# Weight tiles between the steps of a dilated head: 2, 3, 2, 4 and 3 of them in place of 2 each

## What is computed

```
def dilated_layer(x, g, w_in, w_mem_kv, w_out, mem_n, kv):
    h = rmsnorm_2(x, g)
    parts = split_cols(h @ w_in, [DIL_W] * n_g + [DIL_W, MEM_W, MEM_W])
    gate_d, mq, gate_m = parts[n_g], parts[n_g + 1], parts[n_g + 2]
    for gi, (window, dil) in enumerate(DIL_CONFIG):
        q = parts[gi].reshape(B, S, DIL_HEADS, DIL_DH)
        o, lse = dilated_group(q, kv[2 * gi], kv[2 * gi + 1], dil, window // dil)
        outs.append(o); lses.append(lse)
    alpha = jax.nn.softmax(jnp.stack(lses, axis=0), axis=0)
    o = jnp.sum(alpha[..., None] * jnp.stack(outs, axis=0), axis=0)
    o_dil = o.reshape(B, S, DIL_W).astype(x.dtype) * jax.nn.silu(gate_d)
```

## Time and profile before

| | us |
|---|---|
| median of 3 runs | 4379.09 |
| lowest, highest | 4377.94, 4389.87 |
| the profiled execution, its own time | 4371.75 |
| its span in the trace | 4369.9 |
| PE busy | 4004.5 (92%) |
| PE weight loads busy (beside PE) | 3762.6 (86%) |
| ACT busy | 1564.4 (36%) |
| DVE busy | 1510.8 (35%) |
| POOL busy | 1351.6 (31%) |

### The profile page before, as it was taken

One profiled execution on the slowest core, in us unless ns is written; L12 is line 12 of the kernel. 1 busy time (PEld: TensorE's weight loads), 2 busy tenths in 40 slices (PEclk: granted clock), 3 DMA queues, 4 the chain that ended last, 5 costly groups with the idle time before them and its releaser, 6 DMA issues.

```text
span 4369.9 us, 95432 instructions
## 1 busy us (share of the span) xinstructions
PE 4004.5 (92%) x42564; PEld 3762.6 (86%) x42564; DVE 1510.8 (35%) x2011; ACT 1564.4 (36%) x1954; POOL 1351.6 (31%) x632
## 2 busy tenths in 40 slices
PE   6988999889897899999988999898999999999978
PEld 5876778788886899999988999797899999999978
DVE  2123224466655433332333233324222222222232
ACT  3332224521213343343433333334333333333333
POOL 2321113100002344444433344433333333333333
PEclk8999999999998999999999999999999999999989
DMA  5886665100003455555544444444544444445433
GB/s 210 298 287 237 245 229 176 55 4 4 4 10 111 140 183 183 180 188 183 181 145 147 146 154 150 137 158 142 172 158 157 164 149 146 160 157 166 145 123 133
DMA packets 181879, 668.39 MB, mean 153 GB/s; under 512 B 20288, under 2 KB 20288, under 8 KB 180704
## 3 DMA queue, kind: packets, MB, share of 16 engines
q1 hardware_dynamic: 175248, 642.07, 43.0%
q10 hardware_dynamic: 4944, 16.03, 1.1%
q0 software_dynamic: 1280, 4.20, 0.2%
HBM read 653.82 MB, written 8.39 MB: 152 GB/s over the span
## 4 chain that ended last, share of the span: by engine, by line
PE 83%; DVE 6%; ACT 4%; issue 3%; DMA 2%; POOL 1%; ACTq 0%; POOLq 0%; DVEq 0%; SPq 0%
PE ps L903 65%; PE ps L864 2%; PE ps L1144 2%; PE ps L1120 2%; ACT wh L1371 1%; PE ps L1056 1%; PE ps L1134 1%; DVE wl L1833 1%; PE ps L846 1%; PE ps L1359 1%; ACT halves L1371 1%; DMA raw<-in_w_k 1%; POOL wl L2375 1%; PE ps L1343 1%; ACT xw L1371 1%
## 5 line engine op out<-in xcount | busy, mean ns | idle before, releaser
L903 PE MATMUL ps<-halves,wh 128*128 128x256 f32 (+1 forms) x13632 | 2627.1, 294 | 99.3 <-POOL wl L2375 23.2
L903 PEld LDWEIGHTS ps<-halves,wh 128*128 128x128 f32 x13632 | 2185.4, 195 | 170.3 <-issue 80.0
L903 PE MATMUL ps<-halves,wl 128*128 128x256 f32 (+1 forms) x6816 | 1984.7, 291 | 0.0
L2375 POOL TENSOR_TENSOR wl<-raw,wh 128x1024 fp32r<-128x1024 f32 x508 | 1234.2, 2430 | 2121.1 <-ACT wh L1371 2120.8
L1371 ACT ACTIVATE wh<-raw 128x1024 fp32r<-128x1024 f32 x1016 | 1071.9, 1057 | 1493.1 <-PE ps L903 1181.7
L1833 DVE TENSOR_TENSOR wl<-raw,wh 128x1024 fp32r<-128x1024 f32 x508 | 688.4, 1356 | 1919.3 <-ACT wh L1371 1918.9
L903 PEld LDWEIGHTS ps<-halves,wl 128*128 128x128 f32 x6816 | 1328.2, 195 | 14.1
L903 PE MATMUL ps<-wh,halves 128*128 128x256 f32 x2688 | 499.3, 285 | 0.6 <-POOL wl L2375 0.6
L903 PEld LDWEIGHTS ps<-wh,halves 128*128 128x128 f32 x2688 | 424.3, 192 | 11.3 <-issue 8.1
L903 PE MATMUL ps<-wl,halves 128*128 128x256 f32 x1344 | 381.0, 283 | 0.0
L903 PEld LDWEIGHTS ps<-wl,halves 128*128 128x128 f32 x1344 | 258.8, 193 | 0.3
(11 more groups left out here) (243 smaller groups left out, 2488.0 us busy)
## 6 DMA issues: line engine op xcount, KB each, us to landing
raw<-in_ffn SPq DMA_DIRECT2D x264, 512.0 KB, 4.0
raw<-in_ada SPq DMA_DIRECT2D x192, 512.0 KB, 4.6
raw<-in_w_kv SPq DMA_DIRECT2D x192, 512.0 KB, 3.4
raw<-in_w_in_b SPq DMA_DIRECT2D x160, 512.0 KB, 3.9
raw<-in_w_in_a SPq DMA_DIRECT2D x128, 512.0 KB, 3.5
raw<-in_mem SPq DMA_DIRECT2D x64, 512.0 KB, 5.7
raw<-in_w_out_a SPq DMA_DIRECT2D x48, 512.0 KB, 4.0
raw<-in_w_out_b SPq DMA_DIRECT2D x48, 512.0 KB, 4.0
```

The source lines that it names most:

```text
L903: p = self.e.matmul(o, x, y, start=bi not in begun, stop=final and kc == 3 and m == 2, skip_group_check=True)
L2375: return self.e.tensor_tensor(out, a, b, op)
```

## The change

`pipeline_tight` no longer alternates two tiles and one step. A new function deals the tiles of the first seven results by a list of counts that it repeats: two ahead of step 1, three ahead of step 2, two ahead of step 3, four ahead of step 4, three ahead of step 5, and the same for the second head, 28 in all. Tiles, instructions, buffers and banks are the same.

```diff
+def weave(g, steps, counts):
+
+    for n in itertools.cycle(counts):
+        rest(limited(g, n))
+        if next(steps, "end") == "end":
+            break
+    rest(g)
@@
-                run_all((part(made[:7]), 2), (before, 1))
+                weave(part(made[:7]), before, (2, 3, 2, 4, 3))
                 rest(part(made[7:]))
```

## The result

| | before | with the change |
|---|---|---|
| median, us | 4378.51 (4 runs, 4375.6 to 4389.87) | 4351.53 (4 runs, 4348.59 to 4353.76) |
| ratio, 95% interval | | 0.9931 (0.9914 to 0.9948) |
| the profiled execution, its own time | 4371.75 | 4353.76 |
| its span | 4369.9 | 4352.0 |

The change makes the kernel faster: 27 us by the two medians, which is 0.62%, and 0.69% by the ratio in the table, which is not that of the medians. The forecast was 4350.5 us, 28.6 us less than before. Run again later the changed kernel gave 4352.27 us against 4383.85 (6 and 11 runs), a ratio of 0.9929 (0.9913 to 0.9945).

A forecast was written before the change was run, and what follows sets the result against it. TensorE, busy 92%, bounds the kernel, so only its gaps can yield time. 21.1 + 7.5 = 28.6 us off 4371.75 gives 4343.2; the median, 7.3 us above, gives 4350.5 us, range 4335 to 4372.

The forecast's parts named there:

- waits, 28: PE's waits before the transposes in seven pairs of dilated heads: 9.70 to 6.68 us a pair, 21.1 us gained.
- clock: Beside the seven pairs, half-clock stretches of 1.5 us each fall from seven to two: 7.5 us back.
- The late softmax: Dilated heads: softmax begins within the last tile before the transposes (waits 1.97, 2.88 us); more tiles alone cover nothing.
- The rival by which tiles cover a wait: Dilated heads: waits covered by their tiles, as their number suggests; all 67.9 + 10.5 us go, 4301 us; 2%.
- Parity: Dilated heads: new counts make the last split before each softmax POOL's, not DVE's; one DVE `wl` less directly in the way.
- The held multiply: Dilated heads' softmax: DVE's multiply is held until 0.22 us (narrow) or 0.42 us (wide) after POOL's `wl` ends.
- The single waits: A pair's four waits before the transposes become 1.80, 1.54, 1.35 and 1.99 us, from 1.97, 2.88, 1.97 and 2.88.

The follow-up runs named there:

- the even counts: The kernel before with only the list of tile counts ahead of the steps changed, to 2, 4, 2, 4, 2: 4392.36 us, ratio 1.0028.
- the exchange of the low halves: The kernel before, two tiles ahead of every step, with DVE making `wl` of this stage's odd tiles and POOL of the even ones: 4348.00 us, ratio 0.9916.
- the change again: The changed kernel run once more, unaltered, for a narrower interval: 4352.27 us, ratio 0.9929.
- the multiply on ACT: The changed kernel with the softmax's multiply done by ACT (Copy with a scale for each row) instead of DVE: 4322.46 us, ratio 0.9863.
- early softmax, new counts: The changed kernel with the dilated heads' softmax moved into the step of its scores, ahead of the tiles: 4303.49 us, ratio 0.9818.
- early softmax, old counts: The kernel before, two tiles ahead of every step, with the dilated heads' softmax moved into the step of its scores: 4302.47 us, ratio 0.9820.

## Why the prediction was right

| term | forecast, us | measured in the stage, us |
|---|---|---|
| waits, 28 | 21.1 | 68.1 - 45.6 = 22.5 |
| clock | 7.5 | 10.5 (the rest of 33.0), seven stretches of 1.5 |
| sum | 28.6 | 33.0 |

**The late softmax.** Right: the even counts kept both waits, 1.96 and 2.88 us, with twice the tiles, and moving the softmax ahead of the tiles took all of them away. The rival by which tiles cover a wait would have given 4301 us; that time was reached only when the softmax was moved.

**Parity.** Right, and enough by itself: the exchange of the low halves gave the whole gain with the old counts.

**The held multiply.** Right, from the two held instructions of earlier stages, one of them a multiply. Without it the forecast would have been 4311 us. The multiply ends 0.22 us (narrow) and 0.41 to 0.42 us (wide) after POOL, and 0.22 and 0.42 were taken. The Trainium skill (SBUF — State Buffer, "Who interferes with whom") puts such a wait down to an exclusive lock on a pair of SBUF ports that DVE and GpSimd share. The rows of the change and of the exchange agree: every multiply that met POOL's `wl` was held to its end.

**The single waits.** The narrow one behind an eviction was forecast 1.80 and is 1.73, the wide one 1.99 and 1.94. Most of the excess is POOL's duration: it starts 1.19 us after the start of a split behind an eviction, as forecast, and is 2.36 us long, not 2.41, so its end comes 3.55 us after that split's start, not 3.60.

**The clock.** Undersized. Two stretches at half clock were to stay, counting 2 in 14 from the waits of 1.97 us; none did, in two profiled executions of the change (56 waits of up to 1.94 us) and one of the exchange (28 of up to 1.54). The direction was right, the step failed in its size: 10.5 us came back for 7.5. By the even counts, 13 stretches fell beside the same 28 waits that had seven before, 12 of them behind wide ones. Each count is from one trace; that the even counts are slower than the kernel before in 7 and 10 runs too (1.0009 to 1.0047) speaks for the order of the program and against chance in one execution. Either way a forecast can't count on the number that it finds. What decides within one size of wait was not tried and stays open.

**The sum against the runs.** The stage gave 33 us, 4.4 more than forecast, and the medians gave 27 and 31.6 us (4383.85 - 4352.27). The scatter of the rest of the program is larger than these differences. That the forecast, 4350.5 us, lies 1 us from the measured 4351.53 is therefore luck; what is borne out is the four waits, each within 0.07 us, and the direction of the clock.

## What to carry to other kernels

Where every engine runs one interleaved program, ask where in its own queue the waiting work stands, before asking how long it is covered: work issued behind the last filler isn't hidden by any number of fillers. Issue it right behind what it reads, and put the fillers between its result and the reader of that result. Where DVE and POOL share elementwise work, look which DVE operation will run beside POOL's: here one that reads two SBUF streams (`wl`, 2.58 us for 1.23) and an fp32 multiply from SBUF to SBUF (1.90 for 0.42) ended only after the `wl` that POOL had begun. Put such an operation elsewhere or on ACT.

## What the hardware showed that was not expected

The part of the kernel outside the stage, the span less the stage, took 3421.2 us in the profiled execution of before (4369.9 - 948.7) and 3436.3, 3441.6, 3442.1, 3439.4, 3432.9, 3439.4 and 3429.9 in those of the change, the change again, the even counts, the exchange, the multiply on ACT and the early softmax with the new and the old counts. The instructions ahead of the stage are the same in all of these (in the exchange, low halves change hands from 144 us ahead of the stage on), and behind the stage only the eighth pair's differ. The same code thus took up to 21 us more or less, about 0.5%, nearly twice the scatter of the three runs shown ahead of the prediction (12 us); the later runs of the kernel before spread as far, from 4372.52 to 4394.14.

The traces show where the difference arises. The table has, in us, the moment at which the stage begins and the time for which TensorE was granted half clock ahead of it:

| | stage begins | at half clock |
|---|---|---|
| before | 3216.6 | 249 |
| early softmax, old counts | 3223.9 | 259 |
| multiply on ACT | 3226.0 | 266 |
| change | 3231.6 | 290 |
| exchange | 3233.4 | 297 |
| early softmax, new counts | 3234.2 | 287 |
| even counts | 3235.9 | 307 |
| change again | 3236.9 | 297 |

The start of the stage differs by 20 us, and it goes with the time at half clock. Against the trace of before, six of the other seven have more than half of their delay between 722 and 1511 us. Why the clock falls there more often in one execution than in another is not shown. A single execution's time is no measure of a change of 30 us; the stage is one, steady to 0.2 us between the two executions of the change (915.7 and 915.9).
